# Moving the convolution projections of a hybrid attention block in between the attention's query tiles, with normalised probabilities and a raw weight ring of two slots

## The reference

```python
h = modulate(rmsnorm(x, norm1_g), sh1, sc1)
p = h @ w_in                       # kv latent, rope key, q latent, conv x, conv B, conv C, two gates
pr = softmax(s * scale)            # 8 heads, 512 queries, 768 keys
o = einsum('bhqk,bkhd->bqhd', pr, v)
y_conv = (b_gate * dwconv(c_gate * x_in, conv_w, conv_b)) @ w_conv_out   # width 3, 512 channels
y_attn = o @ w_attn_out
x = x + g1 * ((sigmoid(p_ga) * y_attn + sigmoid(p_gc) * y_conv) @ w_o)
x = x + g2 * conv_ffn(modulate(rmsnorm(x, norm2_g), sh2, sc2), w_up, ..., w_down)
return rmsnorm(x, final_g)
```

## Time and profile before

| | us |
|---|---|
| median of 3 runs | 885.34 (885.32 to 887.03) |
| span of the profiled execution | 883.6 |
| the median less this span (what lies around it) | 1.7 |
| attention, 138.17 to 245.48 | 107.3 |
| convolution projections, 245.48 to 311.19 | 65.7 |
| merge, 311.19 to 441.75 | 130.6 |

### The profile page before, as it was taken

The page is one execution under the profiler, slowest core; times in us unless marked ns, Lnnn a source line. Parts: engine busy times, 40 slices in busy tenths (PEclk is TensorE's granted clock), DMA queues, the critical chain, the costliest instruction groups (busy, mean ns, idle before and its releaser), DMA issues.

```text
span 883.6 us, 11658 instructions
## 1 busy us (share of the span) xinstructions
PE 828.0 (94%) x3976; PEld 680.0 (77%) x3976; DVE 451.6 (51%) x560; ACT 376.4 (43%) x580; POOL 376.2 (43%) x191
## 2 busy tenths in 40 slices
PE   5679968999899999999999899999999999999995
PEld 4458856888688888888858798888888888888884
DVE  5853797888723257666423566555555555100014
ACT  6763445778622323222234355444444444211134
POOL 0095352466235445746532335444444444444420
PEclk9979989999999999999999899999999999999998
DMA  8923210011032469856552214333333332322202
GB/s 291 331 64 70 67 48 1 1 48 26 25 90 73 147 194 282 253 176 194 165 166 72 72 29 139 97 97 100 100 100 99 95 95 95 96 96 95 71 1 95
DMA packets 126239, 96.22 MB, mean 109 GB/s; under 512 B 13468, under 2 KB 111033, under 8 KB 126201
## 3 DMA queue, kind: packets, MB, share of 16 engines
q1 hardware_dynamic: 126169, 95.71, 36.0%
q10 hardware_dynamic: 32, 0.01, 0.0%
HBM read 93.60 MB, written 2.10 MB: 108 GB/s over the span
## 4 chain that ended last, share of the span: by engine, by line
PE 77%; DVE 10%; issue 4%; ACT 3%; DMA 3%; POOL 1%; SPq 1%; ACTq 0%; DVEq 0%
PE ps L340 24%; PE ps L342 24%; PE ps L341 24%; DVE small L972 2%; POOL ht L488 1%; PE ps L1357 1%; DVE work L949 1%; DMA xt<-x_dram 1%; PE ps L1346 1%; PE ps L1437 1%; DVE work L953 1%; DVE klo L940 1%; DMA xt<-ctx_dram 1%; DMA raw<-w_in_dram 1%; SPq L223 1%
## 5 line engine op out<-in xcount | busy, mean ns | idle before, releaser
L279 POOL TENSOR_TENSOR wlo<-raw,whi 128x1024 fp32r<-128x1024 f32 (+2 forms) x131 | 306.2, 2342 | 392.2 <-ACT whi L271 391.7
L340 PE MATMUL ps<-hhi,whi 128*128 128x512 f32 (+1 forms) x648 | 251.1, 388 | 8.0 <-DVE hlo L889 4.8
L341 PE MATMUL ps<-hlo,whi 128*128 128x512 f32 (+1 forms) x648 | 249.2, 385 | 0.0
L342 PE MATMUL ps<-hhi,wlo 128*128 128x512 f32 (+1 forms) x648 | 248.9, 384 | 0.0
L271 ACT ACTIVATE whi<-raw 128x1024 fp32r<-128x1024 f32 (+2 forms) x148 | 144.6, 988 | 107.5 <-PE ps L342 88.7
L340 PEld LDWEIGHTS ps<-hhi,whi 128*128 128x128 f32 x648 | 123.5, 191 | 34.0 <-DVE hlo L889 4.8
L342 PEld LDWEIGHTS ps<-hhi,wlo 128*128 128x128 f32 x648 | 123.7, 191 | 23.7
L341 PEld LDWEIGHTS ps<-hlo,whi 128*128 128x128 f32 x648 | 123.7, 191 | 23.5 <-issue 0.5
L1154 DVE SCALAR_TENSOR_TENSOR work<-ps,prm,work 128x511 f32<-128x511 f32 x44 | 33.0, 749 | 76.8 <-ACT work L812 75.9
L1025 DVE SCALAR_TENSOR_TENSOR adacc<-ada,cvec,adacc 128x1024 f32<-128x1024 f32 x28 | 62.2, 2236 | 15.6 <-DMA ada<-w_ada_dram 15.5
L340 PE MATMUL ps<-fhi,whi 128*128 (+1 forms) x176 | 69.2, 393 | 0.1
(11 more groups left out here) (232 smaller groups left out, 1253.1 us busy)
## 6 DMA issues: line engine op xcount, KB each, us to landing
raw<-w_up_dram SPq DMA_DIRECT2D x88, 256.0 KB, 3.1
raw<-w_in_dram SPq DMA_DIRECT2D x66, 256.0 KB, 3.5
ada<-w_ada_dram SPq DMA_DIRECT2D x32, 512.0 KB, 4.7
raw<-w_down_dram SPq DMA_DIRECT2D x44, 256.0 KB, 2.7
raw<-w_ada_dram SPq DMA_DIRECT2D x32, 256.0 KB, 4.7
raw<-w_o_dram SPq DMA_DIRECT2D x16, 256.0 KB, 3.2
xt<-x_dram SPq DMA_DIRECT2D x4, 512.0 KB, 7.0
raw<-w_attn_out_dram SPq DMA_DIRECT2D x8, 256.0 KB, 3.6
```

What stands on the lines that cost most here:

```text
L279: ins = (engine or nc.gpsimd).tensor_tensor(out=l, in0=r, in1=h.bitcast(F32), op=ALU.subtract)
L340: pe.matmul(o, l[0], r[0], start=start, stop=False)
L341: pe.matmul(o, l[0], r[1], start=False, stop=False)
L342: return pe.matmul(o, l[1], r[0], start=False, stop=stop)
```

## The change

1. The 24 matmuls of each convolution projection are cut into pieces (`CONV_PIECES`) of 8 or 12. In every query tile one piece follows `scores(g+2)`, into bank 7. Products, taps and gate follow at fixed tiles. The results go to odd columns of `qhi`, `qlo` instead of `zhi`, `zlo`.
2. Each tile's probabilities are multiplied in place by the inverse of their row sum (`normalize`) before they are transposed; `inverse`, `diagonals`, `row_factors` and the second multiplication of `output_value` go.
3. New keys take a turn in the two bank pairs of the scores (`turn`, `key_turn`), as bank 6 now holds the output; their weights stay in `nhi`, `nlo`.
4. `raw` has two slots instead of four (`RAW`); `whi` and `wlo` keep four. The w_ada units at the start have four slots of their own (`adaraw`).
5. The splits of the convolution's weights are spread over the tiles (`SPLIT_AT`). All 32 `ada2` additions are in the merge, four a tile; their loads start after the last head.

```diff
+RAW = 2
-CONV_SPLITS = (9, 13, 17, 21)
+CONV_PIECES = ((0, 8), (0, 8), (0, 8), (1, 8), (1, 8), (1, 8), (2, 12), (2, 12))
+SPLIT_AT = {1: 2, 4: 3, 6: 4, 9: 5, 12: 6, 14: 7, 17: 8, 20: 9, 22: 10, 25: 11, 28: 12, 30: 13, 31: 14}
-        raw = sb("raw", [P, SLOTS, UNIT])
+        raw = sb("raw", [P, RAW, UNIT])
+        def turn(g):
+            return g + min(HEADS // 2 - 1, (g + 3) // 8)
+        def key_turn(pair):
+            return 9 * pair - 4
         def load(sp, u, slot, pieces):
-            wait(sp, w_lo, u - SLOTS + 1)
+            if not isinstance(u, int) or u >= U_Q + RAW:
+                sp.wait_ge(w_lo, u - RAW + 1)
...
+            for n in range(3):
+                gate_load(0, n)
+            sp.wait_ge(s("pv_ps"), 2 * HEADS)
+            for d in range(DT):
+                for g in range(4):
+                    load_ada2(4 * d + g, d, g)
+                    if g < 3 and d + 1 < DT:
+                        gate_load(d + 1, g)
...
+            for n in range(2):
+                split_hi(act, U_CONV + n, n)
             exps(0)
             exps(1)
...
+                if g in SPLIT_AT:
+                    split_hi(act, U_CONV + SPLIT_AT[g], SPLIT_AT[g] % SLOTS)
+                if g % 8 == 2:
+                    conv_x_copy(g // 8)
+                if g % 8 == 5:
+                    conv_mid(g // 8)
+                if g % 8 == 0 and g > 0:
+                    conv_hi(g // 8 - 1)
...
+            def normalize(g):
+                dve.wait_ge(s("p_exp"), g + 1)
+                nc.vector.reciprocal(inv_sum(g), exp_sum(g)).then_inc(s("p_inv"), 1)
+                dve.wait_ge(s("p_inv"), g + 1)
+                nc.vector.tensor_scalar(probs(g), probs(g), inv_sum(g), None, ALU.mult).then_inc(s("p_norm"), 1)
             for g in range(HEADS * TT):
                 if g + 2 < HEADS * TT:
                     maxima(g + 2)
-                if t == 2:
-                    inverse(h)
+                if g + 1 < HEADS * TT:
+                    normalize(g + 1)
...
+                if g % 8 in (5, 6, 7):
+                    (conv_product, conv_taps, conv_gate)[g % 8 - 5](g // 8)
...
-                    for m in range(3):
-                        nn = 3 * dd + m
-                        ada2_add(8 + 12 * i + nn, 2 + 3 * i + nn // 4, nn % 4)
+                    for m in range(4):
+                        ada2_add(4 * d + m, d, m)
...
             def transposes(g):
-                pe.wait_ge(s("p_exp"), g + 1)
+                pe.wait_ge(s("p_norm"), g + 1)
...
+            def conv_piece(g):
+                j, (n, count) = g // 8, CONV_PIECES[g % 8]
+                at = sum(c for m, c in CONV_PIECES[:g % 8] if m == n)
+                u = U_CONV + 3 * j + n
+                if at == 0:
+                    unit(u)
+                    if n > 0:
+                        pe.wait_ge(s("c_x" if n == 1 else "c_prod"), j + 1)
+                    elif j > 0:
+                        pe.wait_ge(s("c_z"), j)
+                for i in range(at, at + count):
...
                 if g + 2 < HEADS * TT:
                     scores(g + 2)
+                conv_piece(g)
...
-                    row_factors(h - 1)
```

More of the change, by code:

```diff
@@ L290, in query_ready @@
                 used(e, U_UQ + h // 2)
-        def keys_ready(e, pair, part):
-            if (pair, part) == (HEADS // 2 - 1, 1):
-                used(e, U_N)
-            else:
-                e.wait_ge(s("k_ps"), 2 * pair + part + 1)
         flat = work[:].rearrange("p a n -> p (a n)")
@@ L381, in _ @@
                 k, at = (u - U_ADA) // 2, (u - U_ADA) % 2 * D
-                load(sp, u, u % SLOTS, [(raw[:, u % SLOTS, n:n + 512], w_ada[k * P:(k + 1) * P, at + n:at + n + 512])
-                                        for n in (0, 512)])
+                wait(sp, w_lo, u - SLOTS + 1)
+                for n in (0, 512):
+                    sp.dma_start(adaraw[:, u % SLOTS, n:n + 512],
+                                 w_ada[k * P:(k + 1) * P, at + n:at + n + 512]).then_inc(ada_loaded[u % SLOTS], 16)
                 if u % 2 == 1 and u // 2 < KT:
@@ L681, in output_part @@
                 act.wait_ge(s("pv_ps"), 2 * h + 2)
[L682 to L683 removed]
+                wait(act, s("o_lo"), h - 1)
+                nc.scalar.activation(work[r, 0, :], ps[VDIM:P, 6, :], ACT.Copy).then_inc(s("o_part"), 1)
             def output_hi(h):
@@ L1289, in keys @@
                 lo, hi = ((0, T), (T, K))[part]
[L1290 to L1293 removed]
+                if pair == 0:
+                    wait(pe, s("k_raw"), part)
+                    o = ps[:, 6, 0:hi - lo]
+                else:
+                    o = ps[:, 2 * (key_turn(pair) % 2) + part, 0:hi - lo]
+                    if part == 0:
+                        turn_free(pe, key_turn(pair))
                 for k in range(KVT):
[L1295 to L1297 removed]
+                    w = tuple(t[:, k * 512 + pair * P:k * 512 + (pair + 1) * P] for t in (nhi, nlo))
+                    last = mm3(pe, o, w, (ckhi[:, k, lo:hi], cklo[:, k, lo:hi]), k == 0, k == KVT - 1)
+                last.then_inc(s("k_ps"), 1)
             pe.wait_ge(s("ck_lo"), KVT)
@@ L1356, in output @@
                     for n, p_ in enumerate((pthi, ptlo)):
-                        last = pe.matmul(ps[:, 7, q], vs[:, kt, h, :], p_[:, kt, q], start=kt == 0 and n == 0,
+                        last = pe.matmul(ps[:, 6, q], vs[:, kt, h, :], p_[:, kt, q], start=kt == 0 and n == 0,
                                          stop=kt == KT - 1 and n == 1)
@@ L1394, in _ @@
                 output(HEADS - 1, 1, part)
-            row_factors(HEADS - 1)
-            for j in range(CT):
-                for n in range(3):
-                    u = U_CONV + 3 * j + n
-                    unit(u)
-                    wait(pe, s("c_z"), j - 1)
-                    project(pe, ps[:, 3 * (j % 2) + n, :], u % SLOTS, hhi, hlo).then_inc(w_used, 1)
             def merge(i, first):
@@ L1427, in merge @@
                             (qhi[:, 2 * k, :], qlo[:, 2 * k, :]), k == 0, k == CT - 1)
-                    project(pe, ps[:, b + 3, :], slot, zhi, zlo, kt=CT, k0=CT).then_inc(w_used, 1)
+                    for k in range(CT):
+                        last = mm3(pe, ps[:, b + 3, :], (tile_of(whi, slot, CT + k), tile_of(wlo, slot, CT + k)),
+                                   (qhi[:, 2 * k + 1, :], qlo[:, 2 * k + 1, :]), k == 0, k == CT - 1)
+                    last.then_inc(w_used, 1)
             merge(0, True)
```

257 lines of the change are left out of this document (127 added, 130 removed).

## The result

The changed kernel takes 907.79 us (median of 4 runs, 907.26 to 911.2) against 885.54 us (4 runs, one more than above) for the kernel before on the same chip: ratio 1.026, 95% interval 1.0237 to 1.0282. It is slower by 2.6%, where 865 was forecast. The span of its profiled execution is 906.3 us.

A forecast was written before the change was run, and what follows sets the result against it. PE, busy for 94% of the span, was taken as the bound. Stretch -21.5, merge with w_o +1.5, ring 0 and start -0.7 sum to -20.7: span 883.6 to 862.9, plus 1.7 around it, 865 us; range 860 to 876.

The forecast's parts named there:

- Amount of work: First scores to merge: 146.4 us of PE work, the stretch taking 151.5 us instead of 173.0, so -21.5.
- Everything else that a tile waits for now has 4.6 us to come about [...] So I expect small waits only.: Attention tiles with convolution laid in: 4.6 us a tile instead of 3.4, so 3 us of further PE waits.
- The clock: Sign of being wrong: PE's clock in the new stretch falls below the 0.98 of before; no price given.
- Another of its signs: Sign of being wrong: ACT waits long for raw weights in the merge or up projection; no size given.
- The one that it put first: Sign of being wrong: PE waits for the normalisation or the differences in most tiles; no size given.
- Being held by POOL: First scores to merge: POOL holds DVE, notably its normalisation, about 3 us a head; DVE needs 17, below PE's 18.3.
- The ring of two. Cost 0.: Raw weight loads: a round of 7.5 us fits in 10.9 us of PE work for two units, so cost 0.
- Merge and fourth addition: Merge: PE's work unchanged, fourth addition a tile narrowly hidden, 1.7 us before PE; 1.5 us put at w_o (0 to 4).
- The start: Before the first scores: two weight loads in flight instead of four, issued sooner; -0.7 us (0 to -1.4).
- DVE pays POOL's whole time: Rival, first scores to merge: DVE needs 22.5 us a head, 182 us against 173; kernel 895 us, chance 0.04.
- DVE sets the pace: Rival, first scores to merge: meetings with POOL bunch up, 19 to 20 us a head; 871 us (868 to 879), chance 0.16.
- The merge or the ring gives it back: Rival, merge: slow landings stretch the ring's round, fourth addition misses its tile; 8 to 14 us, 870 to 878, chance 0.11.

The follow-up runs named there:

- e12: e10 with the gate of the last tile of each eight placed ahead of the maximum in DVE's list: 866.53 us, ratio 0.9798 to the kernel before.
- e1: Changed kernel with the three readers of bank 7 (product, gate, copy of x) moved earlier in DVE's and ACT's lists: 881.78 us, ratio 0.9974.
- e9: Changed kernel with the edits of e1, e5 and e7 together: 870.65 us, ratio 0.9848 to the kernel before.
- e7: e1 with the small product of maximum and scale computed by ACT instead of DVE: 876.12 us, ratio 0.9899 to the kernel before.
- e4: Kernel before with only the raw ring of two and separate slots for the first w_ada units: 903.32 us, ratio 1.0198.
- e5: e1 with the first three units of w_o loaded between the last four modulation rows: 878.40 us, ratio 0.993 to the kernel before.
- e10: e9 with the convolution piece of the last tile of each eight issued ahead of the scores: 869.74 us, ratio 0.9841 to the kernel before.
- e11: Changed kernel with the small product on ACT and early w_o loads, readers of bank 7 left late: 895.31 us, ratio 1.013 to the kernel before.

## Why the prediction was wrong, point by point

**Amount of work.** Nearly right. PE's work is 151.2 us by e12 and not 146.4, as the prices were taken from groups that don't follow transposes. The gain of the stretch can be had: e12 has -19.5 where -21.5 was forecast. DVE's 17 us a head were measured (135.7 / 8), though not made up as forecast (below).

**"Everything else that a tile waits for now has 4.6 us to come about [...] So I expect small waits only."** This is the step that failed. It compared sums and the chain of attention, and left out the wait for a buffer of the convolution: twelve units share bank 7 one after the other, so that PE can't begin a unit before the reader of the one before it has run. When that is was not a question of DVE's 14 or 17 us a head but of the reader's place in the list: last in a step that runs to the end of its tile. Cost: eight waits, 20.9 us, where 3 were given to everything. With the clock behind them they are 35.5 of the 40.1 us between 151.5 and 191.6, and e1 gave 26.4 back by moving three entries alone. The change was described with products, taps and gate "at fixed tiles"; at which place in the tile was never asked.

**The clock.** The prediction named a clock below 0.98 as a sign of its being wrong and gave it no price. Eight falls cost some 14.6 us more. The kernel before had one in attention (the 0.98 of the earlier trace rows), 0.4 us behind a wait of 0.91. Another of its signs showed too: ACT waited 11.16 us for a raw unit at the end of the merge. The one that it put first, PE waiting for the normalisation, never did.

**Being held by POOL.** The mechanism was named, for the normalisation, and its sum of 3 us a head was about right, in part by luck. Most of it falls elsewhere: the 32 normalisations take 27.4 us where 0.62 each would make 19.8, 7.6 more; the small product of maximum and scale, which took 7.4 us in attention before, takes 26.8 us for 32 times 128 elements, 19.4 more. Together that is 27.0 us, 3.4 a head. Moving the small product away was worth 8.2 us of the stretch (e9 against e1; 6.6 in e7, with a fall).

**"The ring of two. Cost 0."** Wrong. The argument looked at the round of load, ACT and POOL against a unit's PE work, which holds, and not at what else is queued: on SP, behind the waiting load; on ACT, behind the split that waits for it. In the kernel before the same ring costs 19 us (e4). In the changed one 4.4 are lost at w_o, and reordering three loads gave back 3.1 (e5 against e1), which leaves that stage as it was before. No run gives the changed kernel four slots, so the ring's own part in the 4.4 is argued from this and not measured.

**Merge and fourth addition.** +1.5 forecast; the merge is +1.3 and the addition was hidden with 3.9 us to spare. The start: -0.7 forecast, -1.6 read, but kernels with this same start reached the first scores at 135.8 to 139.9 us, so neither figure is measured.

**The rivals.** "DVE pays POOL's whole time" ended on the right side at 895 for a wrong reason: DVE never needed the 21.6 us a head from which it decides, and DVE stood idle for 29% of the stretch. The actual mechanism, a wait for a single buffer whose reader is late by its place, was in none of them. "DVE sets the pace" says that a tile may be over 2 us late before PE notices: in the kernel after PE noticed at eight of the 11 hand-overs. "The merge or the ring gives it back" had the ring's price in the kernel before (19 us, e4), but through the rows and not through the round of load, ACT and POOL.

## What to carry to other kernels

When work is laid into the gaps of a paced loop, adding up engine loads says only what is possible; for every buffer that the new work reuses, write down where its reader stands in the in-order list of its engine, and what each entry ahead of it waits for. Put readers of a single buffer first in their step, ahead of entries that wait for a later product of the same producer, and change producer and reader together (the producer alone gave nothing in e10, with the reader 3.5 us of the stretch in e12).

A ring made shorter must be costed for everything behind the waiting entry on each queue it passes through, most of all transfers that belong to another ring.

## What was unexpected of the hardware

- A wait of PE costs more than its length. In the changed kernel the clock stood at its lower level for 3.4 us, once 6.8, at each of eight waits of 2.3 to 3.4 us; in e1, whose waits are 0.6 to 1.7 us, it didn't fall in the stretch. The length alone doesn't decide: e5 has e1's waits and a fall behind the first, of 1.52 us, and in e11 two waits of 2.29 us had no fall and three of 1.84 to 1.88 had one. One fall of 3.4 us made a stretch of the same instructions 1.6 us longer.
- PE's groups of matmuls right behind six transposes took some 0.08 us longer than the same groups elsewhere (0.80 against 0.71, 1.13 against 1.06), which adds up when each tile has such a place.
- The length of a DVE instruction says nothing of what it can lose to POOL: 128 elements took 2.36 us behind a split of 2.39, and 32 such products took 26.8 us, 16 of them held, most to within 0.02 us of the end of POOL's instruction. Taking them off DVE shortened its busy time by 17.6 us (134.7 to 117.1).
- A sum and a difference of 0.69 us took 2.58 and 2.43 us at the end of the merge, while POOL's splits, late by some microseconds, ran beside them; with three loads reordered they were at 0.69 again.
